# Indexer products of an attention kernel: plain 4-byte operands, two heads on the row halves of the array

## The reference, cut to what matters

```
dots  = einsum('bqhd,bsd->bqhs', qi, ki) * 64 ** -0.5      # 8 heads of 64, one shared key
score = einsum('bqhs,bqh->bqs', relu(dots), wi)            # weighted sum over the heads
score = where(admissible, score, -1e30)
_, idx = top_k(score, topk)                                # 128 of 512 keys; 72 of 288 for samples
```

## Time and profile before

| | |
|---|---|
| Time, median of 3 runs | 627.63 us (625.99 to 630.16) |
| Span of the profiled execution | 625.3 us |
| Time of the profiled execution as a whole | not listed apart; the three runs lie 0.7 to 4.9 us above the span |
| TensorE busy | 598.3 us, 96% of the span, 4462 matmuls |
| VectorE busy | 328.4 us, 53% |
| ScalarE busy | 258.0 us, 41% |
| GpSimd busy | 91.2 us, 15% |
| Mean granted clock of TensorE | 0.989 |

### The profile page before, as it was taken

How to read it: one execution, slowest core, us unless ns; L and a number is a source line. 1 busy time by engine, 2 the same in 40 slices (tenths; PEclk the granted TensorE clock), 3 DMA queues, 4 the chain that set the end, 5 groups by cost and what they waited for, 6 DMA issues and landing times.

```text
span 625.3 us, 10445 instructions
## 1 busy us (share of the span) xinstructions
PE 598.3 (96%) x4462; PEld 551.5 (88%) x4462; DVE 328.4 (53%) x611; ACT 258.0 (41%) x396; POOL 91.2 (15%) x82
## 2 busy tenths in 40 slices
PE   4699999999999999999999999979999999999998
PEld 3699999999778788879979788759999999999997
DVE  4614545788778784756764454438444222344331
ACT  5332545443786667720364334335222222213110
POOL 3701000200322317222400000123000000000000
PEclk9799999999999999998999999998999999999999
DMA  8622224062012020005342210210332223345511
GB/s 240 189 90 69 77 73 135 2 207 68 23 46 68 2 68 0 1 1 160 115 149 68 67 35 1 69 34 1 102 100 70 81 57 100 102 135 169 170 45 39
DMA packets 58175, 50.47 MB, mean 81 GB/s; under 512 B 4304, under 2 KB 53840, under 8 KB 58128
## 3 DMA queue, kind: packets, MB, share of 16 engines
q1 hardware_dynamic: 58128, 49.79, 26.2%
HBM read 42.82 MB, written 6.82 MB: 79 GB/s over the span
## 4 chain that ended last, share of the span: by engine, by line
PE 89%; ACT 4%; DVE 2%; DMA 1%; issue 1%; POOL 1%; SPq 0%; DVEq 0%; ACTq 0%
PE PS L490 35%; PE PS L750 13%; PE PS L765 8%; PE PS L782 7%; PE PS L640 5%; PE PS L474 3%; PE PS L689 3%; PE PS L582 3%; PE PS L612 2%; PE PS L552 2%; PE PS L649 1%; DMA tm<-in_x_prompt 1%; PE PS L617 1%; PE PS L708 1%; PE PS L786 1%
## 5 line engine op out<-in xcount | busy, mean ns | idle before, releaser
L1101 DVE TENSOR_TENSOR wlo<-raw,whi 128x2048 fp32r<-128x2048 f32 (+2 forms) x39 | 79.3, 2033 | 109.0 <-ACT whi L833 108.6
L490 PE MATMUL PS<-whi,xhi 128*128 128x256 f32 x384 | 110.6, 288 | 2.5 <-ACT q_flat L863 1.1
L490 PE MATMUL PS<-wlo,xhi 128*128 128x256 f32 x384 | 109.1, 284 | 0.0
L490 PE MATMUL PS<-whi,xlo 128*128 128x256 f32 x384 | 108.6, 283 | 0.0
L490 PEld LDWEIGHTS PS<-whi,xhi 128*128 128x128 f32 x384 | 73.1, 190 | 4.7 <-ACT q_flat L863 1.3
L750 PE MATMUL PS<-xhi,whi 128*128 128x272 f32 x256 | 74.5, 291 | 0.4 <-issue 0.4
L750 PE MATMUL PS<-xlo,whi 128*128 128x272 f32 x256 | 74.4, 291 | 0.0
L750 PE MATMUL PS<-xhi,wlo 128*128 128x272 f32 x256 | 74.2, 290 | 0.0
L490 PEld LDWEIGHTS PS<-whi,xlo 128*128 128x128 f32 x384 | 73.3, 191 | 0.0
L490 PEld LDWEIGHTS PS<-wlo,xhi 128*128 128x128 f32 x384 | 72.9, 190 | 0.0
L490 PE MATMUL PS<-xhi,whi 128*128 128x272 f32 (+1 forms) x208 | 63.0, 303 | 4.0 <-POOL xlo L1524 3.4
(11 more groups left out here) (207 smaller groups left out, 1272.8 us busy)
## 6 DMA issues: line engine op xcount, KB each, us to landing
raw<-in_w_in SPq DMA_DIRECT2D x18, 1024.0 KB, 5.5
raw<-in_w_in SPq DMA_DIRECT2D x16, 512.0 KB, 4.6
raw<-in_w_o SPq DMA_DIRECT2D x4, 1024.0 KB, 6.4
tm<-in_x_prompt SPq DMA_DIRECT2D x4, 512.0 KB, 6.4
out<-vals SPq DMA_DIRECT2D x2, 1024.0 KB, 4.4
out<-tm SPq DMA_DIRECT2D x2, 1024.0 KB, 7.6
raw<-in_w_a_out SPq DMA_DIRECT2D x8, 256.0 KB, 3.1
raw<-in_w_b_out SPq DMA_DIRECT2D x8, 256.0 KB, 3.4
```

Source lines behind the costliest of these rows:

```text
L490: mm = pe.matmul(out, lhsT, rhs, start=(k == 0), stop=(k == 23))
L1101: dve.tensor_tensor(wlo[:, uu % 2, 0:n], raw[:, uu % 2, 0:n], whi[:, uu % 2, 0:n].bitcast(F32), ALU.subtract).then_inc(w_lo, 1)
```

## The change

The rounded and remainder parts of the indexer's queries and keys go. `iq` is a view of the first half of `q_flat` that holds a pair of heads on 128 partitions, one head on each row half, as the transposes leave them, and `ik` is a view of `kT` with the same key on both halves. Each item is one whole copy on one engine: even items on ScalarE, odd items on VectorE. A dot is one plain 4-byte matmul over 64 partitions, those of its head; `DOTS` now alternates the two heads of a pair, block by block, so that neighbours lie on different halves. A group of `kb0` or `kb1` follows after every four dots as before. The relu and the accumulation keep their form; the accumulation waits for the same block of the head before.

```diff
-ITEM_ON_ACT = [n >= 7 and (15 <= n < 23 or n % 2 == 0) for n in range(len(ITEMS))]
+ITEM_ON_ACT = [15 <= n < 23 or n % 2 == 0 for n in range(len(ITEMS))]
...
-DOTS = [(h, b) for h in range(H) for b in SCORED]
+DOTS = [(2 * p + r, b) for p in range(PAIRS) for b in SCORED for r in range(2)]
...
-        iq_flat = sb_at("iq_flat", H * NT, F32R, at_q)[:, :]
-        iqT = iq_flat[:, 0:H * SEQ].rearrange("p (h n) -> p h n", h=H)
-        iqS = iq_flat[:, H * SEQ:H * NT].rearrange("p (h n) -> p h n", h=H)
-        ikT = sb_at("ikT", 2 * KEYS, F32R, at_k)[:, :].rearrange("p (c n) -> p c n", c=2)
+        iq = q_flat[:, 0:PAIRS * NT].rearrange("p (c n) -> p c n", c=PAIRS)
+        ik = kT[:, 0, :]
...
-            for h in range(H):
-                for n in range(len(SCORED) * h, len(SCORED) * (h + 1)):
-                    b = DOTS[n][1]
-                    if n >= 6:
-                        pe.wait_ge(relu_done, n - 5)
-                    m, q, k0 = (DEC, iqS[:, h, :], SEQ) if b == "s" else (P, iqT[:, h, P * b:P * b + P], 0)
-                    for c in range(2):
-                        mm = pe.matmul(ps[0:m, n % 6, 0:n_keys(b)], q, ikT[:, c, k0:k0 + n_keys(b)],
-                                       start=(c == 0), stop=(c == 1))
-                    mm.then_inc(dot_done, 1)
-                group(FIRST_GROUP[U["kb0"]] + h)
+            for n, (h, b) in enumerate(DOTS):
+                if n >= 6:
+                    pe.wait_ge(relu_done, n - 5)
+                r = HD * (h % 2)
+                m, q0, k0 = (DEC, SEQ, SEQ) if b == "s" else (P, P * b, 0)
+                pe.matmul(ps[0:m, n % 6, 0:n_keys(b)], iq[r:r + HD, h // 2, q0:q0 + m], ik[r:r + HD, k0:k0 + n_keys(b)],
+                          start=True, stop=True).then_inc(dot_done, 1)
+                if n % 4 == 3:
+                    group(FIRST_GROUP[U["kb0"]] + n // 4)
...
+                if kind == "iq":
+                    return eng.activation(iq[:, p, 0:SEQ], bank, ACT.Copy)
+                if kind == "iqs":
+                    return eng.activation(iq[:, :, SEQ:NT], bank[:, 0:PAIRS * DEC].rearrange("p (c n) -> p c n", c=PAIRS), ACT.Copy)
+                if kind == "ik":
+                    return eng.activation(ik[:, 0:SEQ], bank, ACT.Copy)
+                if kind == "ikx":
+                    return eng.activation(ik[:, SEQ:KEYS], bank[:, 0:SKEYS], ACT.Copy)
...
+                if kind == "iq":
+                    last = dve.tensor_copy(iq[:, p, 0:SEQ], bank)
...
-                    dve.wait_ge(acc_done, n - 3)
+                    dve.wait_ge(acc_done, DOTS.index((h - 1, b)) + 1)
```

More of the change, by code:

```diff
@@ L288, in build @@
         item_act = sem("item_act")
-        item_hi = sem("item_hi")
         q_zero = sem("q_zero")
@@ L902, in item_out @@
                 bank = ps[:, ITEM_BANK[n], :]
-                if kind in ("iq", "aq"):
+                if kind == "iq":
[6 more added lines that the diff above has]
+                    return eng.activation(ik[:, SEQ:KEYS], bank[:, 0:SKEYS], ACT.Copy)
+                if kind == "aq":
                     eng.activation(qT[0:HD, 2 * p, 0:SEQ], bank[0:HD, :], ACT.Copy)
                     return eng.activation(qT[HD:P, 2 * p + 1, 0:SEQ], bank[HD:P, :], ACT.Copy)
-                if kind in ("iqs", "aqs"):
+                if kind == "aqs":
                     v = bank[:, 0:PAIRS * DEC].rearrange("p (c n) -> p c n", c=PAIRS)
@@ L909, in item_out @@
                     return eng.activation(qS[HD:P, 1:H:2, :], v[HD:P], ACT.Copy)
-                if kind in ("ik", "bk", "ak"):
+                if kind in ("bk", "ak"):
                     return eng.activation(kT[:, p, 0:SEQ], bank, ACT.Copy)
@@ L923, in _ @@
             for n in I_ITEMS:
[L924 to L938, removed]
+                item(n)
             w_high(U["vb0"] + 2)
             evacuate_unit("vb1")
[L941 to L950, removed]
+            for n, (h, b) in enumerate(DOTS):
+                act.wait_ge(dot_done, n + 1)
+                if n >= 4:
+                    act.wait_ge(acc_done, n - 3)
+                m = DEC if b == "s" else P
+                act.activation(wk[0:m, n % 4, 0:n_keys(b)], ps[0:m, n % 6, 0:n_keys(b)], ACT.Relu,
+                               scale=HD ** -0.5).then_inc(relu_done, 1)
+                if n % 4 == 3:
+                    evacuate(FIRST_GROUP[U["kb0"]] + n // 4)
             for g in range(FIRST_GROUP[U["kb0"]] + H, LAST_GROUP[U["kb1"]] + 1):
@@ L1192, in item @@
                 bank = ps[:, ITEM_BANK[n], :]
-                if kind in ("iq", "aq"):
+                if kind == "iq":
+                    last = dve.tensor_copy(iq[:, p, 0:SEQ], bank)
+                elif kind == "iqs":
+                    last = dve.tensor_copy(iq[:, :, SEQ:NT], bank[:, 0:PAIRS * DEC].rearrange("p (c n) -> p c n", c=PAIRS))
+                elif kind == "ik":
+                    last = dve.tensor_copy(ik[:, 0:SEQ], bank)
+                elif kind == "ikx":
+                    last = dve.tensor_copy(ik[:, SEQ:KEYS], bank[:, 0:SKEYS])
+                elif kind == "aq":
                     dve.tensor_copy(qT[0:HD, 2 * p, 0:SEQ], bank[0:HD, :])
                     last = dve.tensor_copy(qT[HD:P, 2 * p + 1, 0:SEQ], bank[HD:P, :])
-                elif kind in ("iqs", "aqs"):
+                elif kind == "aqs":
                     v = bank[:, 0:PAIRS * DEC].rearrange("p (c n) -> p c n", c=PAIRS)
@@ L1199, in item @@
                     last = dve.tensor_copy(qS[HD:P, 1:H:2, :], v[HD:P])
-                elif kind in ("ik", "bk", "ak"):
+                elif kind in ("bk", "ak"):
                     last = dve.tensor_copy(kT[:, p, 0:SEQ], bank)
```

## The result

The changed kernel takes 631.62 us (median of 4 runs, 631.45 to 632.22), the kernel before 627.82 in the same comparison (4 runs, 625.99 to 630.16): ratio 1.0056, 95% interval 1.0030 to 1.0081. It is slower by half a per cent, inside the forecast range and in the forecast direction. The profiled execution took 631.73 us, with a span of 629.7 us, 4.4 more than before's 625.3.

What follows compares the result with a forecast made beforehand. TensorE, busy for 96% of the span, was taken as the bound. Dots 9.7 + 0.8 + 3.2 + 0.5 = 14.2 us against 10.5, +3.7, less 1.0: +2.7, time 630.3 us; range 625.0 to 636.0.

Steps and rivals of the forecast that it cites:

- The main case: Row halves overlap, shape changes cost TensorE time, the transposes' wait goes: +2.7 us, 630.3 us; chance 0.56.
- the wait at L534: The ikx transposes wait until item 0 is read from PSUM bank 0; this wait goes, -1.0 us.
- the sum: All terms on TensorE's stream: dots 14.2 us against 10.5, +3.7, less 1.0 for the wait, +2.7 us.
- the clock: Rival: TensorE's clock falls in the dots' stage while half its rows idle, costing tens of microseconds; chance 0.02.
- The evacuations: Reading out the seven indexer items: fewer ScalarE and VectorE instructions end the ikx transposes' wait, -1.0 us.
- Beyond the wait this is worth nothing: Fewer evacuation instructions on ScalarE and VectorE gain nothing more than the 1.0 us at the transposes.
- The cover that I named: Between the transposes and the first dot, 73.61 to 87.67, lies all of vb1, covering the remaining evacuations.
- The streaming: Dots as plain products at 1.69 ns per column, two heads side by side on the row halves: 9.7 us.
- 19.4 us: Rival: the row halves don't overlap, so eight heads stream one after the other; 639.2 us, chance 0.17.
- The stagger: In each quad of dots the second half starts 0.1 us late, awaiting its weights: 0.8 us for 8 quads.
- The shape changes: Switching the array around each quad costs 0.4 us, 3.2 for eight; narrowing to 32 columns adds 0.5 us.
- The other engines at nothing: In the dots' stage, relus, accumulations, low parts, zeroing and loads on the other engines don't delay TensorE.

Runs made afterwards that it cites:

- the larger comparison: The changed kernel again, unaltered, against the kernel before with many runs of both in one session: 631.57 us against 628.97, ratio 1.0046.
- the small item first: The kernel before with only its item list reordered, iqs first, so that ikx reuses the bank of iqs: 628.09 us, ratio 0.9990.
- the heads in turn: The changed kernel with the dots in the old order, head by head, so a quad's four dots share one row half: 641.71 us, ratio 1.0202.
- A longer stream with the old operands: The kernel before with the first chunk of each head's first dot multiplied twice, 8 more single-pass products: 631.44 us, ratio 1.0043.
- the form with a stream 1.0 us shorter: The kernel before with iqs first in the items and vb1's first evacuation ahead of the weight copy on ScalarE: 627.98 us, ratio 0.9988.

## Why the prediction was right, and where it was not

The main case was right: the halves overlap, the shape changes eat more than the overlap leaves, and the wait at L534 goes. The forecast time, 630.3, was 1.3 us low. That its +2.7 us fits the +2.6 of the larger comparison is luck: the edits gave +1.5, 1.2 less than the sum, and the clock, which the sum left out, gave back about as much.

- **The evacuations, -1.0 us.** Measured -1.03. "Beyond the wait this is worth nothing" was wrong by the trace of the small item first: with the wait gone and ScalarE's 12 instructions kept, 0.58 us came back as a wait of `vb1`. The cover that I named was the first dot, and I did not look at the bank that `vb1`'s third group needs.
- **The streaming, 9.7 us.** Right; 19.4 us would have been 10 us later, as the heads in turn show.
- **The stagger, 0.8 us.** Wrong. The second half starts 0.007 us after the first in the records, and not 0.1, so it is 0.06 us for eight quads. The unhidden first load is there once, for both halves: the first records of a quad are followed by the next after 0.53 us, where records of the same width later follow after 0.42.
- **The shape changes, 3.2 and 0.5 us.** The stretches take 11.8 us, the groups behind them 0.16 to 0.17 us more each, together +2.6 over before, where the sum had +3.7. Without the stagger it had +2.9, so this term was 0.3 us too large; the quads of 1.70 us were given as about 2.0, with the changes of the neighbouring groups in them. One narrowing is 0.15 us, and a quad's change there and back about 0.3 (0.35: 11.8 us and the 1.3 behind the quads, less 9.7 of streaming and 0.6 of narrowings, over eight).
- **The clock, left at nothing.** This term was missing from the sum. I had the clock as a rival, but with another mechanism, half of the rows at work in the stage of the dots, and there it is at 1.00. What differs is how long it is at the lower level near 290 and 420 us, where neither kernel has an edit. That cost about 2.4 us between the two profiled executions, of which before's is among its fastest, and about 1 us in the median of the larger comparison (2.6 less the edits' 1.5). A longer stream with the old operands shows it too. That the shift alone decides it is not shown: the mix of clocks differs between runs of one kernel, the form with a stream 1.0 us shorter lost the highest clock as well, and no run here sets it.
- **The other engines at nothing.** Right: relus, accumulations and the weights' low part held nobody up.

## What to carry to other kernels

Two products of 64 rows on the two row halves run as one, but each trip from full-array work to halves and back costs 0.3 to 0.4 us and each narrowing 0.15: count the trips before the columns. Putting products of one shape together saves trips, but only where the evacuations leave room for it: here one wait ate more than three trips saved. Where half of a plain product's cost comes back by overlap and the old form was already as cheap, the gain is in what is no longer evacuated, and by the traces a reordered item list with one evacuation moved gives that alone (the intervals of its time still reach 1). And for kernels that differ by under 1%, put the mean clock beside every time, take many runs of both, and check by position in the traces: here the clock 170 us behind the edits moved the time by as much as the edits did, and equal means can hide different stretches.

## What was not expected of the hardware

- A plain 4-byte product over 64 rows costs the same 1.7 ns per column as one over 128 rows, and two of them on the row halves start 7 ns apart, where the products on column halves in the earlier trace rows start 0.08 to 0.21 us apart.
- The price of a change of shape is partly paid by the next full-array matmuls: 3.04 us for 24 of them and not 2.88.
- A thin stretch of TensorE work (24 sample products of 32 columns, 48 records in 4.6 us) is followed or overlapped by 1.2 GHz for 3.4, 6.8 or 10.2 us in the traces; 6.8 us costs 1.1 to 1.3 us more than 3.4, and 10.2 costs 1.6 to 1.7 more. TensorE is busy for 4.76 of the 4.90 us of that stretch (283.6 to 288.5, clock 1.00), so it is hardly idle ahead of the fall. Splitting it in two was worth more than anything in the indexer, 2.8 us by the medians and 1.8 by the means, with 0.55 of it in the trace from a wait that it fills.
